# Depthwise convolution shared out over three engines, one norm's squares collected first, output in four transfers

## The reference

```python
def rmsnorm(x, w):
    y = xf * lax.rsqrt(jnp.mean(xf * xf, axis=-1, keepdims=True) + EPS)
    return (y * w.astype(jnp.float32)).astype(x.dtype)

def conformer_conv(h, w_pw1, b_pw1, w_dw, b_dw, ln_g, ln_b, w_pw2, b_pw2):
    a, gate = jnp.split(h @ w_pw1 + b_pw1, 2, axis=-1)
    y = a * jax.nn.sigmoid(gate)
    y = lax.conv_general_dilated(y, w_dw[:, None, :], window_strides=(1,),
                                 padding=[(CONV_K // 2, CONV_K // 2)], ...,
                                 feature_group_count=CONV_W) + b_dw      # 31 taps along the tokens, each channel by itself
    y = jax.nn.silu(layernorm(y, ln_g, ln_b))
    return y @ w_pw2 + b_pw2
```

## Time and profile before

| | us |
|---|---|
| median of 3 runs | 2672.74 |
| profiled execution | 2676.76 |
| its span, first to last instruction | 2674.8 |
| TensorE busy | 2576.0 (96%) |
| VectorE busy | 1549.6 (58%) |
| ScalarE busy | 1013.2 (38%) |
| GpSimd busy | 98.5 (4%) |
| mean granted TensorE clock | 0.977 |
| tap products on TensorE, 160 records | 70.0 |
| taps on VectorE, line 2040, 80 and 72 instructions | 59.3 and 53.4 |

### The profile page before, as it was taken

How to read it: one execution, slowest core, us unless ns; L and a number is a source line. 1 busy time by engine, 2 the same in 40 slices (tenths; PEclk the granted TensorE clock), 3 DMA queues, 4 the chain that set the end, 5 groups by cost and what they waited for, 6 DMA issues and landing times.

```text
span 2674.8 us, 30981 instructions
## 1 busy us (share of the span) xinstructions
PE 2576.0 (96%) x12302; PEld 2047.6 (77%) x12302; DVE 1549.6 (58%) x2584; ACT 1013.2 (38%) x1556; POOL 98.5 (4%) x124
## 2 busy tenths in 40 slices
PE   8999999999999989999988998999999998999998
PEld 6887788887986667888877876788888665788886
DVE  5455676867355656646564355666653998534433
ACT  4344443434335555434344344322322214323323
POOL 0000000000000000000000000011100010000000
PEclk9999999999899999999999998999999999999999
DMA  5322336454121122333333211366642121233331
GB/s 168 111 80 85 89 99 176 150 162 130 53 87 52 56 72 71 97 93 95 91 92 115 91 59 40 121 194 194 194 132 71 56 63 32 86 96 95 97 100 47
DMA packets 283494, 266.83 MB, mean 100 GB/s; under 512 B 13283, under 2 KB 268567, under 8 KB 283351
## 3 DMA queue, kind: packets, MB, share of 16 engines
q1 hardware_dynamic: 266919, 210.33, 25.7%
q0 software_dynamic: 15024, 54.33, 6.9%
q10 hardware_dynamic: 1408, 0.20, 0.0%
HBM read 262.72 MB, written 2.10 MB: 99 GB/s over the span
## 4 chain that ended last, share of the span: by engine, by line
PE 87%; DVE 7%; issue 2%; ACT 2%; DMA 1%; ACTq 0%; POOL 0%; DVEq 0%; POOLq 0%
PE G L2209 70%; PE G L2225 7%; PE M L2277 2%; DVE Y L2040 2%; DVE S L2040 1%; PE M L711 1%; PE M L1117 1%; PE M L772 1%; PE M L782 1%; DVE w_lo L496 1%; PE M L1590 1%; PE M L2259 1%; PE M L1128 1%; PE M L1139 1%; PE M L1579 0%
## 5 line engine op out<-in xcount | busy, mean ns | idle before, releaser
L496 DVE TENSOR_TENSOR w_lo<-raw,w_hi 128x1024 fp32r<-128x1024 f32 x396 | 482.9, 1224 | 683.8 <-ACT w_hi L491 682.6
L2209 PE MATMUL G<-H_hi,w_hi 128*128 128x512 f32 (+1 forms) x2016 | 808.9, 401 | 18.1 <-DVE H_lo L359 9.6
L491 ACT ACTIVATE w_hi<-raw 128x1024 fp32r<-128x1024 f32 x396 | 417.0, 1056 | 994.2 <-PE G L2209 886.9
L2209 PE MATMUL G<-H_hi,w_lo 128*128 128x512 f32 (+1 forms) x2016 | 787.9, 391 | 0.0
L2209 PE MATMUL G<-H_lo,w_hi 128*128 128x512 f32 (+1 forms) x2016 | 787.6, 391 | 0.0
L2209 PEld LDWEIGHTS G<-H_hi,w_hi 128*128 128x128 f32 x2016 | 382.9, 190 | 121.2 <-issue 39.4
L2209 PEld LDWEIGHTS G<-H_lo,w_hi 128*128 128x128 f32 x2016 | 383.1, 190 | 80.3 <-issue 5.9
L2209 PEld LDWEIGHTS G<-H_hi,w_lo 128*128 128x128 f32 x2016 | 382.3, 190 | 80.1
L2209 PE MATMUL G<-hid_hi,w_hi 128*128 128x512 f32 x864 | 339.1, 392 | 5.8 <-DVE hid_lo L615 4.7
L2209 PE MATMUL G<-hid_lo,w_hi 128*128 128x512 f32 x864 | 338.5, 392 | 0.0
L2209 PE MATMUL G<-hid_hi,w_lo 128*128 128x512 f32 x864 | 338.3, 392 | 0.0
(11 more groups left out here) (311 smaller groups left out, 2421.4 us busy)
## 6 DMA issues: line engine op xcount, KB each, us to landing
raw<-in_w_ff SPq DMA_DIRECT2D x128, 512.0 KB
mod_w<-in_w_mod POOLq DMA_DIRECT2D x96, 512.0 KB, 4.5
raw<-in_ffn_w_up SPq DMA_DIRECT2D x176, 256.0 KB
raw<-in_ffn_w_down SPq DMA_DIRECT2D x40, 512.0 KB
raw<-in_w_in SPq DMA_DIRECT2D x28, 512.0 KB
raw<-in_mlstm_w_in SPq DMA_DIRECT2D x24, 512.0 KB
raw<-in_kv_w SPq DMA_DIRECT2D x16, 512.0 KB
raw<-in_fox_w_qg SPq DMA_DIRECT2D x16, 512.0 KB
```

What stands on the lines that cost most here:

```text
L491: act.activation(w_hi[:, j, :], raw[:, j, :], ACT.Copy).then_inc(hi_done, 1)
L496: dve.tensor_tensor(w_lo[:, j, :], raw[:, j, :], w_hi[:, j, :], ALU.subtract).then_inc(lo_done, 1)
L2209: mm = pe.matmul(G[:, 2 * p + m, 0:n], lw[:, k, ms], rh[:, t, 0:n], start=(t == 0 and q == 0), stop=(t == st["ktiles"] - 1 and q == 2), sk ...
```

## The change

- **Convolution.** 31 taps are now 15 on VectorE (`V_TAPS`), ten on TensorE, six on GpSimd (`POOL_TAPS`).
- TensorE's ten taps work on quadrants of the array, 64 rows by 64 columns. Five taps take `yp` as it lies (partitions 0-63 to 0-63, 64-127 to 64-127). The other five take `yp_turned`, a copy of `yp` with the two halves of the partitions exchanged, which ScalarE makes with two copies of 64 x 512 behind the gated product; its products go from one half to the other. A group's products land in two banks of `M` instead of one, and all four banks are in use, so that the column sums move to `G[:, 0]`. There are 20 products of 64 x 64 for each group instead of ten of 128 x 128.
- GpSimd makes the diagonals in two multiplications of 320 elements instead of one of 1280, then six products (tap weight broadcast along the tokens) and five sums of 512 elements, each sum waiting until what it adds is there.
- VectorE adds three things to a group in place of one: the low and the high bank, and GpSimd's sum. `total_low` lies where `total` lay, `total_high` behind the sum of the two accumulators.
- **First norm.** VectorE adds the eight tiles' squares up in SBUF (`collected`), and TensorE sums them over the channels with one product behind the first linear layer, in place of eight within it.
- **Output.** Four transfers of 512 KB, each as soon as its two tiles are there.

```diff
 PE_TAPS = 10
-V_TAPS = CONV_K - PE_TAPS
+HALF_TAPS = PE_TAPS // 2
+POOL_TAPS = 6
+V_TAPS = CONV_K - PE_TAPS - POOL_TAPS
 
...
         yp = at("yp", 112 * K, [P, 2, T + 2 * PAD])
-        tap_diag = at("tap_diag", 117 * K, [P, 2, PE_TAPS, P])
+        tap_diag = at("tap_diag", 117 * K, [P, 2, PE_TAPS, HP])
+        yp_turned = at("yp_turned", 125 * K, [P, 2, T + 2 * PAD])
+        taps_turned = at("taps_turned", 130 * K, [P, 8 * HALF_TAPS])
+        pool_sum = at("pool_sum", 132 * K, [P, 2, T])
+        pool_tap = at("pool_tap", 136 * K, [P, 2, T])
+        half_ident = at("half_ident", 131 * K, [P, HP])
 
...
             ffn2(1)
-            sp.wait_ge(fin_c, 8)
             out_v = out.rearrange("a (b p) d -> p (a b) d", p=P)
-            sp.dma_start(out_v, x_tm[:]).then_inc(done, 16)
-            sp.wait_ge(done, 16)
+            for t in range(1, DT, 2):
+                sp.wait_ge(fin_c, t + 1)
+                part = slice((t - 1) * P, (t + 1) * P)
+                sp.dma_start(out_v[:, :, part], x_tm[:, :, part]).then_inc(done, 16)
+            sp.wait_ge(done, 64)
 
...
                     pe.wait_ge(mod_ok, 4)
-                pe.wait_ge(cv_w, g + 1)
+                pe.wait_ge(cv_w, 2 * g + 2)
                 wait_read(pe, "p_1", g)
+                pe.wait_ge(cv_x, 2 * g + 4)
                 pe.wait_ge(cv_d, g + 1)
-                for j in range(PE_TAPS):
-                    mm = pe.matmul(M[:, 2 + p, :], tap_diag[:, p, j, :], yp[:, p, V_TAPS + j:V_TAPS + j + T],
-                                   start=(j == 0), stop=(j == PE_TAPS - 1))
+                low, high = slice(0, HP), slice(HP, P)
+                for j in range(HALF_TAPS):
+                    here, there = V_TAPS + j, V_TAPS + HALF_TAPS + j
+                    for hs, bank in ((low, 2 * p), (high, 2 * p + 1)):
+                        pe.matmul(M[hs, bank, :], tap_diag[hs, p, j, :], yp[hs, p, here:here + T], start=(j == 0),
+                                  stop=(j == HALF_TAPS - 1), skip_group_check=True)
+                    for hs, other, bank in ((low, high, 2 * p), (high, low, 2 * p + 1)):
+                        mm = pe.matmul(M[other, bank, :], tap_diag[hs, p, HALF_TAPS + j, :],
+                                       yp_turned[hs, p, there:there + T], start=(j == 0), stop=(j == HALF_TAPS - 1),
+                                       skip_group_check=True)
                 mm.then_inc(cv_pe, 1)
...
             linear("p_1", H_hi, H_lo, need=from_h("odd"), behind=taps)
+            wait_read(pe, "p_1", DT - 2)
             for t in range(DT):
                 pe.wait_ge(cv_d, t + 3)
-                mm = pe.matmul(M[:, 1, :], ones[:], Y[:, t, :], start=(t == 0), stop=(t == 7))
+                mm = pe.matmul(G[:, 0, :], ones[:], Y[:, t, :], start=(t == 0), stop=(t == 7))
             mm.then_inc(cv_s, 1)
...
                                bias=VT[:, ds(g + (ROW["b_pw1_2"] + 8), 1)]).then_inc(glu_a, 1)
-
+                wait_read(act, "p_1", g)
+                act.wait_ge(cv_pe, g + 1)
+                for to, hs in ((slice(HP, P), slice(0, HP)), (slice(0, HP), slice(HP, P))):
+                    act.activation(yp_turned[to, p, PAD:PAD + T], yp[hs, p, PAD:PAD + T], ACT.Copy).then_inc(cv_x, 1)
+
+            turned_taps = ROW["w_dw_2"] + 8 * (V_TAPS + HALF_TAPS)
+            for to, hs in ((slice(HP, P), slice(0, HP)), (slice(0, HP), slice(HP, P))):
+                act.activation(taps_turned[to, :], VT[hs, turned_taps:turned_taps + 8 * HALF_TAPS],
+                               ACT.Copy).then_inc(cv_x, 1)
             groups(act, "p_1", split_hi, glu)
...
             dve.wait_ge(chunk_used, used_after("s0_down3"))
+            dve.memset(yp_turned[:], 0.0)
             link(dve.memset(yp[:], 0.0))
...
 
-            def total(g, p):
+            def total_low(g, p):
 
                 dve.wait_ge(cv_pe, g + 3)
-                y = Y[:, ds(g, 1), :]
-                dve.tensor_tensor(y, y, M[:, 2 + p:3 + p, :], ALU.add).then_inc(cv_d, 1)
+                y = Y[:, g, :]
+                dve.tensor_tensor(y, y, M[:, 2 * p, :], ALU.add).then_inc(cv_a, 1)
+
+            def total_high(g, p):
+
+                dve.wait_ge(cv_a, 2 * g + 1)
+                y = Y[:, g, :]
+                dve.tensor_tensor(y, y, M[:, 2 * p + 1, :], ALU.add).then_inc(cv_a, 1)
+                dve.wait_ge(cv_a, 2 * g + 2)
+                dve.wait_ge(cv_g, g + 1)
+                dve.tensor_tensor(y, y, pool_sum[:, p, :], ALU.add).then_inc(cv_d, 1)
 
...
                 if g:
-                    total(g + (-1), 1 - p)
+                    total_low(g - 1, 1 - p)
                 dve.tensor_tensor(y, y, other, ALU.add).then_inc(cv_v, 1)
+                if g:
+                    total_high(g - 1, 1 - p)
                 dve.wait_ge(cv_v, g + 1)
...
             groups(dve, "p_1", split_lo, glu)
-            total(DT - 1, 1)
+            total_low(DT - 1, 1)
+            total_high(DT - 1, 1)
             dve.wait_ge(cv_s, 1)
             for t in range(DT):
-                dve.scalar_tensor_tensor(Y[:, t, :], M[:, 1, :], -1.0 / D, Y[:, t, :], ALU.mult,
+                dve.scalar_tensor_tensor(Y[:, t, :], G[:, 0, :], -1.0 / D, Y[:, t, :], ALU.mult,
                                          ALU.add).then_inc(cv_m, 1)
...
             taps = VT[:, ROW["w_dw_2"]:ROW["w_dw_2"] + 8 * CONV_K].rearrange("p (j t) -> p j t", t=8)
-            for i in range(0, DT // 2):
-                for p in range(2):
-                    pool.wait_ge(cv_pe, i * 2 + (p + 1))
-                    pool.tensor_tensor(tap_diag[:, p], ident[:].unsqueeze(1).to_broadcast([P, PE_TAPS, P]),
-                                       taps[:, V_TAPS:CONV_K, ds(i * 2 + p, 1)].to_broadcast([P, PE_TAPS, P]),
-                                       ALU.mult).then_inc(cv_w, 1)
+            link = Chain(pool, cv_l)
+            turned = taps_turned[:].rearrange("p (j t) -> p j t", t=8)
+            pool.tensor_tensor(half_ident[:], ident[:, 0:HP], ident[:, HP:P], ALU.add).then_inc(cv_h, 1)
+            pool.wait_ge(cv_h, 1)
+            pool.wait_ge(cv_x, 2)
+            each = half_ident[:].unsqueeze(1).to_broadcast([P, HALF_TAPS, HP])
+            for t in range(DT):
+                p = t % 2
+                pool.wait_ge(cv_pe, t + 1)
+                pool.tensor_tensor(tap_diag[:, p, 0:HALF_TAPS], each,
+                                   taps[:, V_TAPS:V_TAPS + HALF_TAPS, t:t + 1].to_broadcast([P, HALF_TAPS, HP]),
+                                   ALU.mult).then_inc(cv_w, 1)
+                pool.tensor_tensor(tap_diag[:, p, HALF_TAPS:PE_TAPS], each,
+                                   turned[:, :, t:t + 1].to_broadcast([P, HALF_TAPS, HP]),
+                                   ALU.mult).then_inc(cv_w, 1)
+                wait_read(pool, "p_1", t)
+                pool.wait_ge(cv_d, t + 1)
+                first = CONV_K - POOL_TAPS
+                if t:
+                    pool.wait_ge(cv_g, t)
+
+                def tap(dst, j):
+                    return pool.tensor_tensor(dst, yp[:, p, j:j + T], taps[:, j, t:t + 1].to_broadcast([P, T]), ALU.mult)
+
+                link.post(tap(pool_sum[:, p, :], first))
+                for j in range(first + 1, CONV_K):
+                    link(tap(pool_tap[:, j % 2, :], j))
+                    one = pool.tensor_tensor(pool_sum[:, p, :], pool_sum[:, p, :], pool_tap[:, j % 2, :], ALU.add)
+                    if j < CONV_K - 1:
+                        link.post(one)
+                one.then_inc(cv_g, 1)
 
...
                     x_turn(t + 4)
-                norm_tiles("pre0", (t,))
                 pe.wait_ge(h_lo, FILL["pre0"] + t + 1)
...
             finish(first)
+            pe.wait_ge(n_ss, 7)
+            pe.matmul(M[:, 0, :], ones[:], SA[:, 0, :], start=True, stop=True).then_inc(n_ss, 1)
             mlstm_pe(pe, linear, linear_units, gate_rows, from_h, squares_behind)
...
                     split_hi(act, 0)
-                if t >= 2:
-                    act.wait_ge(n_ss, 8 * NORM["pre0"] + t - 1)
-                act.activation(SQ[:, t % 2, :], X[:, t, :], ACT.Square).then_inc(n_sq, 1)
+                if t >= 3:
+                    act.wait_ge(n_ss, t - 2)
+                act.activation(SQ[:, t % 2, :] if t else SA[:, 0, :], X[:, t, :], ACT.Square).then_inc(n_sq, 1)
                 if t == 0:
...
             mix_weight = lambda t: vt("norm_mix_pre", t)
+
+            def collected(t):
+                dve.wait_ge(n_sq, t + 1)
+                if t >= 2:
+                    dve.wait_ge(n_ss, t - 1)
+                dve.tensor_tensor(SA[:, 0, :], SA[:, 0, :], SQ[:, t % 2, :], ALU.add).then_inc(n_ss, 1)
+
             x_copy(0)
...
             x_copy(3)
+            collected(1)
             split_lo(dve, 1)
...
                 unscaled_dve(dve, "pre0", mix_weight, t - 2)
+                collected(t - 2)
                 if t in (5, 7):
                     split_lo(dve, t // 2)
```

(9 more changed lines are left out.)

## The result

The changed kernel took **2726.23 us** (median, 2723.34 to 2728.40) against 2673.77 for the kernel before on the same chip: ratio 1.0192, 95% interval 1.0174 to 1.0210, slower by 52 us. Its profiled execution took 2727.44 us with a span of 2725.6, which is 50.8 above the span of before (2674.8).

What follows compares the result with a forecast made beforehand. VectorE and TensorE both full in the convolution stage, with the chain over VectorE. Stage +52.6, behind it +2.5, first norm -4, output -2.5: +48.6 on the median of 2672.74, 2721 us, range 2690 to 2756.

Steps and rivals of the forecast that it cites:

- its main step: Convolution stage, eight groups: VectorE's and GpSimd's times add up, 202 us against 149.4, +52.6.
- GpSimd's operation: Convolution: a product or sum of 512 elements on GpSimd takes 0.94 us, eleven in a group, 10.3 us.
- the first norm: Start of the kernel: seven square sums of 0.86 us leave TensorE, a third lost to VectorE's late half: -4 us (0 to -6).
- The exclusion: Convolution: VectorE's scalar_tensor_tensor taps with two SBUF inputs and GpSimd's SBUF-reading instructions block each other; group 25.7 us.
- one row of 984 ns: Earlier trace: a VectorE instruction of the taps' form, median 748 ns, ended 0.54 us behind GpSimd's products; read as exclusion.
- The first rival: Convolution: the taps don't exclude GpSimd, VectorE bounds at 16.8 us a group, -25.5 with the edges, 2647 us; 12 in 100.
- The group: Convolution of 128 channels: VectorE's 13.2 us plus GpSimd's 11.5 plus 1.0 for waits, 25.7 us against 19.2.
- orders that don't lie ready: Convolution: GpSimd's sums wait for products, so half of VectorE's non-excluding 2.1 us is added to the group, 1.0 us.
- The sum by it: Whole kernel with the skill's estimate of 1.1 us for a GpSimd operation: about 14 us higher, 2735 us.
- TensorE's quadrants four at once: Convolution: 20 products of 64 by 64 on four quadrants together take 4.3 us a group (bounds 4.3 and 17.2).
- Behind the stage: After the convolution: TensorE, idle before, runs the norm's column sums at a lower granted clock, +2.5 us (0 to 6).
- The output: End of the kernel: four transfers of 512 KB land sooner than one of 2 MB, -2.5 us (bounds 0 and 3.5).

Runs made afterwards that it cites:

- experiments 2 and 3: Two kernels against the changed one: gpsimd_writes_only, 2656.25 us; and one whose VectorE scalar_tensor_tensor taps read one input from PSUM, 2664.55 us.
- gpsimd_writes_only: Changed kernel with GpSimd's eleven products and sums replaced by memsets that read nothing: 2656.25 us, ratio 0.9884 to 0.9939.
- experiment 5: Kernel before with the edit of the first norm alone: 2671.61 us, ratio 0.9981 (0.9969 to 0.9994).
- experiment 6: Kernel before with the output in four transfers alone: 2674.30 us, ratio 0.9995 (0.9981 to 1.0009).
- no_gpsimd_taps: Changed kernel with GpSimd's six taps given back to VectorE and its sum left out: 2668.24 us, ratio 0.9961.
- gpsimd_asks_mid_chain: Changed kernel with GpSimd's taps held back until VectorE's fifth tap, signalled by a memset of one column: 2718.75 us, ratio 1.0158.
- the kernel with fourteen: Changed kernel with no taps on GpSimd, 14 on TensorE's quadrants and 17 on VectorE: 2650.68 us, ratio 0.9913 against the kernel before.

## Why the prediction was right

Forecast 2721 us, range 2690 to 2756; measured 2726.2. It held because of its main step. Two of its terms were mis-sized, GpSimd's operation and the first norm, and what made up for them is luck.

- **The exclusion** (forecast: the taps exclude GpSimd, by one row of 984 ns). Right, and shown from both sides by experiments 2 and 3. The first rival's price was right too: without the exclusion a group was to take 16.8 us, and gpsimd_writes_only has 16.9. Its whole kernel is 19 us under before by the medians of its chip and 24 by the ratio, where I had 25.5. What decided between 2647 and 2721 was that one row, and its fit to 0.01 us.
- **The group**, 25.7 us and a stage of 202: measured 26.0 (from the second group on) and 204.9. Terms inside compensate. GpSimd's operation of 512 elements takes 1.04 us and not 0.94 (11 of them, +1.1), the diagonals 0.73 and not 0.59 (+0.3): 12.9 us, with VectorE's 13.2 that is 26.1 where I had 24.7. The 1.0 us that I had added for orders that don't lie ready was not there: GpSimd's orders follow each other without a gap. Instead all of VectorE's other work, 2.1 us, comes on top (GpSimd rests from 2179.45 to 2186.97, when it is done), and 2.2 come back where instructions of the two overlap, 0.13 in each pair of 1.57; where the rest of the 2.2 lies was not worked out. So GpSimd's time was 1.4 us short, and that a wrong 1.0 stood in for it is luck.
- **The Trainium skill's figure and rule.** By 4497 ns for 2048 elements (the Trainium skill, GPSIMD Engine Reference, 3.1) GpSimd's operation is an estimate of 1.1 us, nearer to the measured 1.04 than mine. The sum by it, 2735 us, was not nearer: 2726.2 lies 5 above mine and 9 below it. That a VectorE instruction with two SBUF inputs and a GpSimd instruction that reads SBUF block each other (the Trainium skill, SBUF — State Buffer, "Who interferes with whom") agrees with the traces: taps of 1.52 to 1.78 us beside such instructions, of 0.74 beside memsets or with one input from PSUM.
- **TensorE's quadrants four at once**: right (the earlier trace rows held for quadrants: 0.43 us for four records); twice that where the clock is 0.5. TensorE idles for 8.2 us of the group from 2160, and the granted clock of six groups is 0.81.
- **Behind the stage**, +2.5 (0 to 6): right in size, measured +2.8. But the column sums, which I had named, have only a third of it (the eighth takes 2.1 us at half clock instead of 1.14); the first of the square sums behind them have +1.8.
- **The first norm**, -4 (0 to -6): mis-sized. The start gives 0.7 us in the kernel after, and from -0.8 to 2.2 in the ten traces with this edit. I had named the low half that comes late and taken off a third for it. It took all of the 3.4 us that had gone ahead of it, and the square sums were also what kept TensorE busy: with them gone it pays for its wait with some four microseconds of a clock of 0.52 and 0.62, 1.8 us of the 2.6 that were left. That the stage began 4.3 us early all the same, next to the forecast 4, is luck: 3.6 us are from code that no edit touches, where the trace of before had a low clock (experiment 5).
- **The output**, -2.5: 3.1 in both traces that have it, and not to be told from nothing in experiment 6's time.
- The sum: 55.5 + 2.8 - 4.3 - 0.1 - 3.1 = 50.8, forecast 48.6.

## What to carry to other kernels

Before work is moved from VectorE to GpSimd, look at the inputs of both: where VectorE reads two SBUF tensors and GpSimd reads SBUF, their times add up, and a tap moved here took 1.82 us of the group for the 0.66 that it freed; put one of VectorE's inputs in PSUM or leave GpSimd out. TensorE's quadrants were where the work could go, as long as neighbours in the order of issue lie on different quadrants. And work taken off TensorE ahead of a wait may gain nothing: here it made the wait longer, and in eight of ten traces the granted clock behind it was 0.53 to 0.73. See what else fills that gap first.

## What the runs showed of the hardware

- GpSimd was kept out through eleven of VectorE's taps in an unbroken run: 7.96 us for an operation of 0.73 (no_gpsimd_taps). Where it came in at the first tap (after) or behind a memset of one column (gpsimd_asks_mid_chain), the two alternated at 1.57 us a pair from there on. What lets it in is open.
- tensor_scalar from SBUF waits for GpSimd's memsets also (1.25 us instead of 0.48), scalar_tensor_tensor with two SBUF inputs doesn't.
- Four products of 64 by 64 on different quadrants ran in the time of one (0.43 us a record at a clock of 1.00); the 28 products of a group of the kernel with fourteen, ordered by quadrant, took 19.4 us where four at once need 6.0.
